# Group norm of an SSD scan: summed onto all partitions with a matrix of ones, in place of a column that is spread again

## Chip, cores and metric

One core of a Trainium2 chip. The metric is the device time of one execution in microseconds, median of several runs.

## What is computed

One step of a hybrid decoder layer: 512 prompt tokens and 8 single-token sequences go through a shared RMS norm and input projection, then through two branches, sparse attention and a Mamba-2 scan (SSD), then a gated merge and a feed-forward block. The change is in the scan branch. Its 2048 channels are eight groups of 256; each group's output is multiplied by a gate and then normalised over its own 256 channels:

```python
y = y.reshape(b, t, D_INNER) * jax.nn.silu(z.astype(F32))
yg = y.reshape(b, t, SSM_GROUPS, D_INNER // SSM_GROUPS)
yg = yg * lax.rsqrt(jnp.mean(yg * yg, axis=-1, keepdims=True) + EPS)
y = yg.reshape(b, t, D_INNER) * ssm_norm_w.astype(F32)
```

For the eight sequences a top-k of 256 out of 2049 scores is also needed; it has nothing to do with the scan, but VectorE does its 32 rounds in between.

## The kernel before

Everything is float32 and lies channels on partitions, the T = 520 tokens (512 + 8) in the free dimension. Each engine has its own program written out by hand, with semaphores between them; there is no scheduler, so the order of the lines in an engine's block is its order on the chip. S("name") is a semaphore; counters such as 4 * g + 3 are absolute.

The scan runs over groups g = 0 to 7. Group 0 and group 7 stand alone, 1 to 6 are a hardware loop (Fori). The pass of group g computes group g and, between, (a) the projection tiles of group g + 1 on TensorE: D(0) to D(5), each 128 output channels by 520 tokens over 8 blocks of input channels, 32 records in the profile (16 matmuls, of two records each), and (b) the norm of group g - 1. So seven passes hold a norm, and the eighth norm stands behind the scan.

The norm of a group, before: POOL adds the squares of the two 128-channel halves into sqg. TensorE (step_norm, sum_squares, L387) multiplies each block of tokens with a column of ones, which leaves the sums with tokens on partitions, 4 columns of 128 and one of 8, in PSUM bank 6. ScalarE takes the root of these five columns into rt (root_norm, L403), VectorE inverts them (recip_norm, L409). TensorE visits a second time and spreads them back over all partitions (spread_norm, L395 and L396), ScalarE copies that to rbg (copy_norm, L413 and L414), and VectorE multiplies Y with it (norm, L1651), which gives the group's two tiles of ssm_o.

Around it on TensorE: D(1), the spread, then step_turn, which transposes B (L900) and x (L905; it writes banks 6 and 7, in which the norm's sums lie), then D(2), step_decode (L917, for which it needs VectorE's xdt), D(3), step_cb (L925, C times B, which needs the end of VectorE's decode work on both halves), then the chunks of the scan (L934, L947, L950, L953) between D(4) and D(5). On VectorE, in order: the convolution, four silus (L1675), the reciprocal, MAX8 of a top-k round (L1627), the norm of group g - 1, xdt (L1686), xw, the rest of that round, the decode work (L1706 to L1720), and a second round.

Behind the scan, TensorE turns the state (L1002) and runs the SSM branch's projection over the sixteen tiles of ssm_o (sbr, L359); only its first tile waits for each ssm_o tile as it becomes ready. VectorE does the remaining 16 rounds of the top-k, with a gated product (gated, L1765) after every second one, and TensorE waits for the last round at L1038.

Of the kernel before, what the change touches and what calls it, by code (L numbers as in the profile page):

```python
# [76 lines left out]
def build(nc, x_prompt, x_sample, cache_k, cache_v, cache_idx_k, state_ssm, state_conv, page_table,  # L77
# [5 lines left out]
    with ExitStack() as ctx:  # L83
# [284 lines left out]
        def two(ap):  # L368

            return ap.rearrange("p (h t) -> p h t", h=2)  # L370
# [8 lines left out]

        NORM2, NORMF = NG + 1, NG + 2  # L380

        def sum_squares(pe, e, *squares):

            for b in range(5):
                n = P if b < 4 else NB
                for i, sq in enumerate(squares):
                    mm = pe.matmul(ps[0:n, 6, b:b + 1], sq[:, b * P:b * P + n], ones[:, 0:1],  # L387
                                   start=(i == 0), stop=(i == len(squares) - 1))
            mm.then_inc(S("norm_summed"), 1)
# [59 lines left out]
        def _(sp):  # L449
# [43 lines left out]

            sp.wait_ge(S("iktok_copied"), 2)
            sp.dma_start(ik_prompt[0, 0].rearrange("(b p) d -> p b d", p=P), iktok[:, 0:4, :]).then_inc(S("stored"), 16)
# [164 lines left out]
        def _(pe):  # L660
# [98 lines left out]
            with pe.Fori(0, 2) as k:  # L759
                for s in range(2):  # L760
                    pe.wait_ge(w_in_slot[s], 16 * k + 16)
                    for j in range(2):
                        dense(pe, 4 * k + N_IQ + 2 * s + j, j, block_of(s, j), xns)
            pe.wait_ge(S("ik_sq"), 1)
            for h in range(2):
# [74 lines left out]
            pe.wait_ge(S("kvtok_copied"), 5)  # L840
            pe.wait_ge(S("iktok_copied"), 2)
            pe.wait_ge(S("dense_read"), N_SSM)
# [47 lines left out]
            def step_norm(g):  # L890

                pe.wait_ge(S("sqg_added"), g + 1)
                sum_squares(pe, g + 1, sqg[:, 0, :])

            def step_turn(g, prev):

                pe.wait_ge(S("ctok_ready"), g + 1)
                pe.wait_ge(S("silu_done"), 4 * g + 3)
                for c in range(4):
                    pe.transpose(ps[:, 5, c * P:(c + 1) * P], xc[:, 2, c * P:(c + 1) * P], ident)  # L900
                if prev:
                    pe.wait_ge(S("norm_copied"), 2 * g + 2)
                for c in range(4):
                    for j in range(2):
                        mm = pe.transpose(ps[:, 6 + c // 2, (c % 2) * 256 + j * P:(c % 2) * 256 + (j + 1) * P],  # L905
                                          xc[:, j, c * P:(c + 1) * P], ident)
                mm.then_inc(S("turned"), 1)
# [48 lines left out]
            def group(g, prev, more):  # L956
                D = (lambda *a: group_tile(g + 1, *a)) if more else last_tile
                D(0, 0, 4)
                step_aux(g, prev)
                D(0, 4, 8)  # L960
                if prev:
                    step_norm(g - 1)
                D(1)
                if prev:
                    spread_norm(pe, g)
                step_turn(g, prev)
                D(2)
# [29 lines left out]
            step_norm(NG - 1)  # L997
            spread_norm(pe, NG)
            pe.wait_ge(S("h_done"), 4 * NG)
# [44 lines left out]

            pe.wait_ge(S("norm_copied"), 2 * NG + 2)
            pe.wait_ge(S("decode_read"), POS_READ)
# [104 lines left out]
        def _(act):  # L1151
# [18 lines left out]
            act.wait_ge(S("tensor_mark"), VECS_TURNED)  # L1170
            act.activation(vec[:, 0:72], ps[:, 4, 0:72], ACT.Copy).then_inc(S("vec_ready"), 1)
            copy_norm(act, 0, rbc)
            act.activation(taps, ps[:, 4, 128:256], ACT.Copy, scale=0.5).then_inc(S("taps_ready"), 1)
            act.activation(dsk, ps[:, 4, 256:272], ACT.Copy).then_inc(S("dsk_ready"), 1)
            act.wait_ge(S("dense_done"), 1)
# [7 lines left out]
            act.wait_ge(S("vector_mark"), IK_SQ_IN)  # L1183
            act.activation(ikt2, ikt1, ACT.Square).then_inc(S("ik_sq"), 1)
            with act.Fori(0, 4) as k:
# [5 lines left out]
            act.wait_ge(S("tensor_mark"), IK_VAR)  # L1191
            act.activation(two(ikt2), ps[:, 4:6, 0:TH], ACT.Sqrt, bias=eps[:, 0:1]).then_inc(S("ik_root"), 1)
            act.wait_ge(S("tensor_mark"), TOK_TURNED)
# [33 lines left out]
            act.wait_ge(S("dense_read"), N_SSM)  # L1227
            act.activation(qkvs[:, 0:8, :], uT[:, :, SEQ:T], ACT.Copy).then_inc(S("qkvs_ready"), 1)
            act.activation(qkvs[:, 8:12, :], kviq[:, 0:4, SEQ:T], ACT.Copy).then_inc(S("qkvs_ready"), 1)
            act.wait_ge(S("tensor_mark"), IK_TURNED)  # L1230
            act.activation(iktok[:, 0:4, :], ps[:, 4, 0:256].rearrange("p (b d) -> p b d", b=4), ACT.Copy).then_inc(S("iktok_copied"), 1)
            act.activation(iktok[0:NB, 4, :], ps[0:NB, 4, 256:320], ACT.Copy).then_inc(S("iktok_copied"), 1)
            for b in range(5):
# [62 lines left out]
            def squares(g):  # L1296
                for j in range(2):
                    act.wait_ge(S("Y_ready"), 2 * g + j + 1)
                    act.activation(sqg[:, j, :], Y[:, j, :], ACT.Square).then_inc(S("sqg_ready"), 1)

            def group(g, prev, more):
                for i in range(4):
# [25 lines left out]
                if prev:  # L1328
                    root_norm(act, g, 256)
                if more:  # L1330
                    tile_in(g + 1, 0)
                    tile_in(g + 1, 1)
                else:
                    gate_ahead(0)
                    gate_ahead(1)
                if prev:
                    copy_norm(act, g, rbg)
                act.wait_ge(S("turned"), g + 1)
# [27 lines left out]
            group(NG - 1, True, False)  # L1366
            root_norm(act, NG, 256)
            copy_norm(act, NG, rbg)
            act.wait_ge(S("aux_done"), NG + 1)
# [101 lines left out]
        def _(v):  # L1471
# [10 lines left out]
            v.wait_ge(S("vec_ready"), 1)  # L1482
            rms_dve(v, 0, 0, 0)
# [26 lines left out]
            for c in range(4):  # L1510
# [5 lines left out]
                                   ALU.mult, ALU.add).then_inc(S("vector_mark"), 1)  # L1516
            v.wait_ge(S("ik_root"), 1)
            chain(v.reciprocal(ikt2, ikt2))
# [121 lines left out]
            def z_gate(g):  # L1640

                for j in range(2):
# [3 lines left out]
                    v.scalar_tensor_tensor(z, thz[:, j, :], 1.0, z, ALU.add, ALU.mult).then_inc(S("z_ready"), 1)  # L1646

            def norm(g):
                v.wait_ge(S("norm_copied"), 2 * g + 4)
                for j in range(2):  # L1650
                    v.scalar_tensor_tensor(ssm_o[:, bass.ds(2 * g + j, 1), :].rearrange("p o t -> p (o t)"), Y[:, j, :],  # L1651
                                           cwg[:, bass.ds(g, 1), 22 + j:23 + j].rearrange("p o t -> p (o t)"), rbg,
                                           ALU.mult, ALU.mult).then_inc(S("ssm_ready"), 1)

            def group(g, prev, more):
# [21 lines left out]
                if prev:  # L1677
                    recip_norm(v, g)
                    top_max(GROUP_ROUNDS * g)
                    norm(g - 1)  # L1680
                else:
                    top_max(GROUP_ROUNDS * g)
# [73 lines left out]
            group(NG - 1, True, False)  # L1756
            recip_norm(v, NG)
            norm(NG - 1)


# [102 lines left out]
        def _(g):  # L1863

            g.wait_ge(S("vec_ready"), 1)
            g.wait_ge(S("taps_ready"), 1)
            g.wait_ge(S("dsk_ready"), 1)
            tp = taps.rearrange("p (t n) -> p n t", t=4)
# [156 lines left out]
```

## Time and profile before

| | |
|---|---|
| median of 3 runs | 1772.5 us (1771.49 to 1774.18) |
| the profiled execution: its time, its span | 1774.49 us, 1772.7 us |
| TensorE busy | 1681.0 us, 95% of the span |
| VectorE busy | 767.6 us, 43% |
| ScalarE busy | 401.1 us, 23% |
| GpSimd busy | 217.5 us, 12% |
| mean granted clock of TensorE | 0.96 |

Busy time is summed over the whole span. The scan lies at about 360 to 942 us; one pass takes about 71.4 us. In the rows below the first number is the start in us from the span's start, the second the time in us; "x32" counts records that were merged into one row, and a bracket gives the idle time of that engine ahead of the row and what ended it. PE is TensorE, DVE is VectorE, ACT is ScalarE.

### The profile page before, as it was taken

How to read it: one execution, taken by the hardware profiler on the slowest of the kernel's cores; microseconds unless marked ns; L12 is line 12 of the kernel's file. 1: busy time of each engine (PE TensorE's matmuls, PEld its weight loads, DVE VectorE, ACT ScalarE, POOL GpSimd, SP SyncE). 2: the span in 40 equal slices, each digit the busy share in tenths (PEclk: the TensorE clock that was granted, in tenths of full speed). 3: DMA queues.
4: the chain of work that ended last, by engine and by line, in shares of the span. 5: the costliest groups of instructions: out<-in, count | busy, mean ns of one | idle time of the engine just before them, and what ended most of it. 6: DMA issues, size and time to landing. Idle time of an engine off the chain costs nothing. (4 is left out here: it accounts for less than half of the span.)

```text
span 1772.7 us, 21861 instructions
## 1 busy us (share of the span) xinstructions
PE 1681.0 (95%) x8411; PEld 1426.5 (80%) x8411; DVE 767.6 (43%) x1192; ACT 401.1 (23%) x855; POOL 217.5 (12%) x224
## 2 busy tenths in 40 slices
PE   6998998999999999999999999999899999999997
PEld 5886786787877878777777888888788888888886
DVE  3314886166776866868657972011210001010002
ACT  3113226223333343343421000101111111110002
POOL 1000111013132241232310005100000000000000
PEclk8998989999999999999899999889899999999997
DMA  6111123223313222131223225112212222222201
GB/s 197 48 36 49 39 61 93 57 65 102 96 55 97 78 69 77 54 101 48 79 72 109 85 72 169 60 57 72 71 52 91 71 71 71 71 68 65 82 1 48
DMA packets 153482, 131.12 MB, mean 74 GB/s; under 512 B 11410, under 2 KB 149938, under 8 KB 153410
## 3 DMA queue, kind: packets, MB, share of 16 engines
q1 hardware_dynamic: 150610, 121.93, 22.7%
q0 software_dynamic: 2816, 8.39, 1.6%
q8 instruction: 42, 0.69, 0.2%
q14 instruction: 14, 0.11, 0.0%
HBM read 117.26 MB, written 13.27 MB: 74 GB/s over the span
## 5 line engine op out<-in xcount | busy, mean ns | idle before, releaser
L359 PE MATMUL ps<-xn,ring 128*128 128x260 f32 x4160 | 951.7, 388 | 7.6 <-DVE xn L442 3.3
L359 PEld LDWEIGHTS ps<-xn,ring 128*128 128x128 f32 x4160 | 793.7, 193 | 136.0 <-issue 3.8
L359 PE MATMUL ps<-work,ring 128*128 128x260 f32 x960 | 210.7, 382 | 0.0
L359 PEld LDWEIGHTS ps<-work,ring 128*128 128x128 f32 x960 | 182.4, 190 | 28.0
L359 PE MATMUL ps<-ssm_o,ring 128*128 128x260 f32 x512 | 114.0, 386 | 0.0
L359 PEld LDWEIGHTS ps<-ssm_o,ring 128*128 128x128 f32 x512 | 98.3, 192 | 15.3
L1834 DVE TENSOR_TENSOR xT<-xT,work 128x520 f32<-128x520 f32 x16 | 11.2, 701 | 192.3 <-ACT work L1434 192.3
L1941 POOL TENSOR_TENSOR ring<-ring 128x512 f32<-128x512 f32 x32 | 40.5, 1266 | 334.2 <-ACT ring L1294 334.2
L1848 DVE SCALAR_TENSOR_TENSOR work<-work 128x520 f32 (+1 forms) x22 | 15.4, 700 | 145.8 <-ACT work L1449 145.8
L1627 DVE MAX8 work<-work 8x8 f32<-8x2049 f32 x32 | 72.9, 2278 | 0.6
L1633 DVE FIND_INDEX8 dix<-work 8x8 uint32<-8x2049 f32 x32 | 72.8, 2274 | 0.0
L1636 DVE MATCH_REPLACE8 work<-work 8x2049 f32<-8x2049 f32 x32 | 72.5, 2267 | 0.0
L1852 DVE TENSOR_TENSOR work<-work 128x520 f32 (+1 forms) x22 | 15.4, 701 | 130.8 <-ACT work L1453 130.8
L1668 DVE SCALAR_TENSOR_TENSOR work<-work 128x512 f32<-128x512 f32 x96 | 67.0, 768 | 7.3 <-ACT work L1304 7.3
L359 PE MATMUL ps<-uT,ring 128*128 128x260 f32 x256 | 59.0, 395 | 0.4 <-DVE uT L1819 0.4
L1735 DVE TENSOR_TENSOR work<-work 128x256 f32<-128x256 f32 x24 | 18.0, 750 | 93.5 <-PE ps L953 93.5
L359 PEld LDWEIGHTS ps<-uT,ring 128*128 128x128 f32 x256 | 50.4, 197 | 8.7 <-DVE uT L1819 0.5
L1290 ACT ACTIVATE ring<-ps,work 128x128 f32<-128x128 f32 x128 | 36.6, 368 | 79.6 <-PE ps L934 79.6
L1434 ACT ACTIVATE work<-ps 128x520 f32<-128x520 f32 x16 | 9.7, 604 | 194.4 <-PE ps L359 194.4
L1264 ACT ACTIVATE work<-ps 128x520 f32<-128x520 f32 x32 | 18.2, 594 | 129.7 <-PE ps L359 129.7
L1453 ACT ACTIVATE work<-ps 128x520 f32<-128x520 f32 x22 | 13.3, 604 | 134.8 <-PE ps L359 134.8
L934 PEld LDWEIGHTS ps<-work,gs 32*128 32x128 f32 x256 | 30.8, 186 | 9.1 <-issue 8.1
(300 smaller groups left out, 1665.2 us busy)
## 6 DMA issues: line engine op xcount, KB each, us to landing
ring<-in_w_in SPq DMA_DIRECT2D x34, 1024.0 KB, 5.3
ring<-in_w_ffn_up SPq DMA_DIRECT2D x11, 1024.0 KB, 5.3
ring<-in_w_ffn_gate SPq DMA_DIRECT2D x11, 1024.0 KB, 5.3
ring<-in_w_in SPq DMA_DIRECT2D x16, 512.0 KB, 5.3
work<-in_state_ssm SPq DMA_DIRECT2D x16, 512.0 KB, 6.3
out<-work SPq DMA_DIRECT2D x16, 512.0 KB, 4.0
ring<-in_w_ssm_br SPq DMA_DIRECT2D x8, 1024.0 KB, 7.9
ring<-in_w_ffn_down SPq DMA_DIRECT2D x8, 1024.0 KB, 5.1
```

Of the source, the lines that this page charges most:

```text
L359: mm = pe.matmul(ps[0:m, 2 * pair + h, 0:TH], lhs[k], rhs[k][:, h * TH:(h + 1) * TH], start=(k == 0), stop=(k == len(lhs) - 1))
L934: mm = pe.matmul(ps[:, 4, r * P:(r + 1) * P], gs[:, r * P:(r + 1) * P], acT[0:32, c * P:(c + 1) * P], start=True, stop=True)
L1264: act.activation(two(raw[:, i, 3:T + 3]), tile_out(i % 2), ACT.Copy).then_inc(S("dense_read"), 1)
L1290: act.activation(M2[:, c % 2, r * P:(r + 1) * P], abc[:, r * P:(r + 1) * P], ACT.Relu, scale=-1.0, bias=atg[:, c, r:r + 1]).then_inc(S("E_ ...
L1627: v.max(dm8[0:NB, :], smp[0:NB, :]).then_inc(S("dtop_max"), 1)
L1633: v.max_index(dix[:], dm8[0:NB, :], smp[0:NB, :]).then_inc(S("dtop_index"), 1)
L1636: v.match_replace(smp[0:NB, :], dm8[0:NB, :], smp[0:NB, :], -3.3e38).then_inc(S("dtop_cut"), 1)
L1668: v.scalar_tensor_tensor(xc[:, i, 0:SEQ], raw[:, i, t:t + SEQ], cw[:, 5 * i + t:5 * i + t + 1], xc[:, i, 0:SEQ], ALU.mult, ALU.add).then_i ...
L1735: v.tensor_tensor(hT.rearrange("p (r q) -> p r q", q=64), hT.rearrange("p (r q) -> p r q", q=64), ealast[:, :, c:c + 1].broadcast_to((P, 4 ...
L1848: v.scalar_tensor_tensor(hs[j], gate[:, j, :], 1.0, hs[j], ALU.add, ALU.mult).then_inc(S("silu_h"), 1)
L1852: v.tensor_tensor(hs[j], hs[j], stage[:, j, :], ALU.mult).then_inc(S("hid_ready"), 1)
L1941: g.tensor_tensor(m, m, CBm[:, c:c + 1, :].broadcast_to((P, 4, P)), ALU.mult).then_inc(S("M_ready"), 1)
```

## The change

The sum of squares is made with the whole 128x128 matrix of ones as the stationary operand, which leaves each token's sum on all 128 partitions, 520 columns in banks 6 and 7. ScalarE takes the root of all 520 columns straight into rbg, VectorE inverts rbg in place, and the spreading and the two copies go. Turning x now waits for the root (group_root), since that frees banks 6 and 7. The norms outside the scan (root_norm, copy_norm, spread_norm with e = 0, NORM2, NORMF) stay as they were. Seven semaphores of the head, each raised by ScalarE, become one, head_read, with counts; that is shown once.

```diff
+        VEC_READY, TAPS_READY, DSK_READY, IK_SQ, IK_ROOT, QKVS_READY, IKTOK_READY = 1, 2, 3, 4, 5, 7, 9
-            v.wait_ge(S("ik_root"), 1)
+            v.wait_ge(S("head_read"), IK_ROOT)
...
             def step_norm(g):
 
                 pe.wait_ge(S("sqg_added"), g + 1)
-                sum_squares(pe, g + 1, sqg[:, 0, :])
+                for h in range(2):
+                    mm = pe.matmul(ps[:, 6 + h, 0:TH], ones, sqg[:, 0, h * TH:(h + 1) * TH], start=True, stop=True)
+                mm.then_inc(S("group_summed"), 1)
...
                 if prev:
-                    pe.wait_ge(S("norm_copied"), 2 * g + 2)
+                    pe.wait_ge(S("group_root"), g)
                 for c in range(4):
                     for j in range(2):
                         mm = pe.transpose(ps[:, 6 + c // 2, (c % 2) * 256 + j * P:(c % 2) * 256 + (j + 1) * P],
...
                 D(1)
-                if prev:
-                    spread_norm(pe, g)
                 step_turn(g, prev)
...
             step_norm(NG - 1)
-            spread_norm(pe, NG)
...
+            def group_norm(g):
+
+                act.wait_ge(S("group_summed"), g)
+                act.activation(two(rbg), ps[:, 6:8, 0:TH], ACT.Sqrt, scale=1.0 / 256,
+                               bias=eps[:, 0:1]).then_inc(S("group_root"), 1)
...
                 if prev:
-                    root_norm(act, g, 256)
+                    group_norm(g)
                 if more:
                     tile_in(g + 1, 0)
                     tile_in(g + 1, 1)
...
-                if prev:
-                    copy_norm(act, g, rbg)
                 act.wait_ge(S("turned"), g + 1)
...
+            def group_recip(g):
+                v.wait_ge(S("group_root"), g)
+                v.reciprocal(rbg, rbg).then_inc(S("group_recip"), 1)
+
             def norm(g):
-                v.wait_ge(S("norm_copied"), 2 * g + 4)
+                v.wait_ge(S("group_recip"), g + 1)
...
                 if prev:
-                    recip_norm(v, g)
+                    group_recip(g)
                     top_max(GROUP_ROUNDS * g)
                     norm(g - 1)
```

How the instructions stand on TensorE in a pass of the loop, from the second half of D(0) to the turning. Before (lines of the kernel before; L387 is the sum, L395 and L396 the spread, L900 and L905 the turning):

```order
L359 MATMUL ps<-xn,ring 128x260 x8
L387 MATMUL ps<-cst,work 128x1 x4
L387 MATMUL ps<-cst,work 8x1
L354 REGISTER_ALU
L359 MATMUL ps<-xn,ring 128x260 x16
L393 ISA
L395 MATMUL ps<-cst,rt 128x128 x4
L396 MATMUL ps<-cst,rt 128x8
L898 REGISTER_ALU
L900 MATMUL ps<-cst,work 128x128 x4
L905 MATMUL ps<-cst,work 128x128 x8
L808 ISA
```

And with the change, where L895 is the sum, L903 and L908 the turning:

```order
L360 MATMUL ps<-xn,ring 128x260 x8
L895 MATMUL ps<-work,cst 128x260 x2
L355 REGISTER_ALU
L360 MATMUL ps<-xn,ring 128x260 x16
L901 REGISTER_ALU
L903 MATMUL ps<-cst,work 128x128 x4
L908 MATMUL ps<-cst,work 128x128 x8
L809 ISA
```

Between D(1) and the turning nothing of the norm is left; the sum in front of D(1) has two instructions of 260 columns in place of five of one.

On VectorE in the same pass, from the silus to the norm. Before:

```order
L1675 SCALAR_TENSOR_TENSOR work<-work 128x520 x4
L409 RECIPROCAL rt<-rt 128x4
L409 RECIPROCAL rt<-rt 8x1
L1625 REGISTER_ALU
L1627 MAX work<-work 8x8
L1649 ISA
L1651 ISA
L1651 REGISTER_ALU
L1651 SCALAR_TENSOR_TENSOR ssm_o<-work,cwg 128x520
L1651 ISA
L1651 REGISTER_ALU
L1651 SCALAR_TENSOR_TENSOR ssm_o<-work,cwg 128x520
```

With the change (L1682 are the silus, L1653 is the reciprocal, L1630 MAX8, L1658 the norm):

```order
L1682 SCALAR_TENSOR_TENSOR work<-work 128x520 x4
L1653 RECIPROCAL work<-work 128x520
L1628 REGISTER_ALU
L1630 MAX work<-work 8x8
L1658 ISA x2
L1658 SCALAR_TENSOR_TENSOR ssm_o<-work,cwg 128x520
L1658 ISA
L1658 REGISTER_ALU
L1658 SCALAR_TENSOR_TENSOR ssm_o<-work,cwg 128x520
```

The reciprocal keeps its place, ahead of MAX8 and the norm, with xdt and xw behind those, and has 520 columns in place of four and one.

On TensorE behind the last group, from the last tile of the scan to the top-k's transposes (L1038 in both). Before:

```order
L359 MATMUL ps<-xn,ring 128x260 x6
L387 MATMUL ps<-cst,work 128x1 x4
L387 MATMUL ps<-cst,work 8x1
L395 MATMUL ps<-cst,rt 128x128 x4
L396 MATMUL ps<-cst,rt 128x8
L1002 MATMUL ps<-cst,work 128x128 x2
L359 MATMUL ps<-ssm_o,ring 128x260 x192
L359 MATMUL ps<-xn,ring 128x260 x32
L359 MATMUL ps<-ssm_o,ring 128x260 x64
L1038 MATMUL ps<-cst,work 128x8 x2
```

With the change:

```order
L360 MATMUL ps<-xn,ring 128x260 x6
L895 MATMUL ps<-work,cst 128x260 x2
L1002 MATMUL ps<-cst,work 128x128 x2
L360 MATMUL ps<-ssm_o,ring 128x260 x192
L360 MATMUL ps<-xn,ring 128x260 x32
L360 MATMUL ps<-ssm_o,ring 128x260 x64
L1038 MATMUL ps<-cst,work 128x8 x2
```

The state's transposes (L1002) and the projection over ssm_o follow the sum directly.

## Rows read from the trace of the kernel before

**Rows 1.** TensorE's timeline in a middle pass: start, us, line, records, idle before.

```profile
653.53 7.28 PE L359 MATMUL ps<-xn,ring 128*128 128x260 f32 x32
663.91 1.16 PE L395 MATMUL ps<-cst,rt 128*128 128x128 f32 x8 [3.10 <-DVE rt L409]
...
666.22 1.91 PE L905 MATMUL ps<-cst,work 128*128 128x128 f32 x8
667.93 7.58 PE L359 MATMUL ps<-xn,ring 128*128 128x260 f32 x32
...
686.37 1.16 PE L925 MATMUL ps<-work 128*128 128x128 f32 x8 [0.27 <-DVE ring L1717]
```

**Rows 2.** ScalarE's timeline in that pass, the root.

```profile
661.92 1.28 ACT L403 ACT_TABLE_LOAD   x1
663.21 0.40 ACT L403 ACTIVATE rt<-ps,eps 128x4 f32<-128x4 f32 x2
```

**Rows 3.** VectorE's timeline in that pass, from the reciprocal to the decode work.

```profile
663.64 0.21 DVE L409 RECIPROCAL rt<-rt 128x4 f32<-128x4 f32 x2 [1.12 <-ACT rt L403]
663.85 2.28 DVE L1627 MAX8 work<-work 8x8 f32<-8x2049 f32 x1
666.37 1.43 DVE L1651 SCALAR_TENSOR_TENSOR ssm_o<-work,cwg 128x520 f32 x2 [0.24 <-ACT work L414]
668.17 1.29 DVE L1686 TENSOR_TENSOR xdt<-ps,work 128x512 f32<-128x512 f32 x2 [0.37 <-PE ps L905]
...
677.40 1.23 DVE L1706 TENSOR_TENSOR ring<-ps,work 128x1024 f32<-128x1024 f32 x1 [1.93 <-PE ps L917]
```

**Rows 4.** Answers on lines L1192 and L1518, both in the head.

```profile
L1192 ACT ACTIVATE work<-ps,eps x1: 695/695/695, 106.3 to 106.3; 128x520 f32<-128x520 f32 x1
...
L1518 DVE RECIPROCAL work<-work x1: 3403/3403/3403, 107.0 to 107.0; 128x520 f32<-128x520 f32 x1
```

**Rows 5.** VectorE's timeline, first and last pass with a norm.

```profile
451.05 2.28 DVE L1627 MAX8 work<-work 8x8 f32<-8x2049 f32 x1
453.56 1.43 DVE L1651 SCALAR_TENSOR_TENSOR ssm_o<-work,cwg 128x520 f32 x2 [0.23 <-ACT work L414]
...
463.32 1.22 DVE L1706 TENSOR_TENSOR ring<-ps,work 128x1024 f32<-128x1024 f32 x1 [1.13 <-PE ps L917]
...
878.31 2.27 DVE L1627 MAX8 work<-work 8x8 f32<-8x2049 f32 x1
...
894.11 1.23 DVE L1706 TENSOR_TENSOR ring<-ps,work 128x1024 f32<-128x1024 f32 x1 [3.65 <-PE ps L917]
```

**Rows 6.** Windows of 3.5 us; TensorE's granted clock is third from the end.

```profile
451.00:454.50 3.50, 3.23 (x24) 2.83 (x25) 3.27 (x5) 1.48 (x5) 0.00 (x0) 1.00 0.92 297
664.50:668.00 3.50, 3.50 (x21) 3.25 (x20) 3.06 (x3) 0.74 (x3) 0.00 (x0) 0.62 0.29 98
880.50:884.00 3.50, 2.84 (x12) 2.65 (x12) 2.34 (x5) 1.20 (x4) 0.00 (x0) 0.50 0.00 0
```

**Rows 7.** TensorE's timeline: D(0)'s second half, and waits for the reciprocal.

```profile
436.22 5.36 PE L359 MATMUL ps<-xn,ring 128*128 128x260 f32 x16
...
451.10 1.16 PE L395 MATMUL ps<-cst,rt 128*128 128x128 f32 x8 [1.40 <-DVE rt L409]
...
649.02 3.67 PE L359 MATMUL ps<-xn,ring 128*128 128x260 f32 x16
...
878.44 1.16 PE L395 MATMUL ps<-cst,rt 128*128 128x128 f32 x8 [1.42 <-DVE rt L409]
```

**Rows 8.** TensorE's timeline behind the last group.

```profile
937.27 1.18 PE L387 MATMUL ps<-cst,work 128*128 128x1 f32 x10 [3.06 <-POOL work L1908]
...
942.20 18.10 PE L359 MATMUL ps<-ssm_o,ring 128*128 128x260 f32 x75
...
1071.77 0.29 PE L1038 MATMUL ps<-cst,work 8*128 8x8 f32 x2 [1.67 <-DVE work L1638]
```

**Rows 9.** VectorE's timeline behind the last group.

```profile
1056.74 0.70 DVE L1765 SCALAR_TENSOR_TENSOR work<-work 128x520 f32<-128x520 f32 x1 [8.79 <-ACT work L1384]
```

More of the change, by code:

```diff
@@ L375, in block_of @@
             return [ring[:, slot, k, j * P:(j + 1) * P] for k in range(kt)]
-        NORM2, NORMF = NG + 1, NG + 2
+        NORM2, NORMF = 1, 2
         def sum_squares(pe, e, *squares):
@@ L492, in _ @@
             sp.dma_start(smp[0:NB, 0:PAST], scratch).then_inc(S("smp_in"), 16)
-            sp.wait_ge(S("iktok_copied"), 2)
+            sp.wait_ge(S("head_read"), IKTOK_READY)
             sp.dma_start(ik_prompt[0, 0].rearrange("(b p) d -> p b d", p=P), iktok[:, 0:4, :]).then_inc(S("stored"), 16)
@@ L763, in _ @@
                         dense(pe, 4 * k + N_IQ + 2 * s + j, j, block_of(s, j), xns)
-            pe.wait_ge(S("ik_sq"), 1)
+            pe.wait_ge(S("head_read"), IK_SQ)
             for h in range(2):
@@ L840, in _ @@
             pe.wait_ge(S("kvtok_copied"), 5)
-            pe.wait_ge(S("iktok_copied"), 2)
+            pe.wait_ge(S("head_read"), IKTOK_READY)
             pe.wait_ge(S("dense_read"), N_SSM)
@@ L1043, in _ @@
             ga(2, 0)
-            pe.wait_ge(S("norm_copied"), 2 * NG + 2)
+            pe.wait_ge(S("group_root"), NG)
             pe.wait_ge(S("decode_read"), POS_READ)
@@ L1170, in _ @@
             act.wait_ge(S("tensor_mark"), VECS_TURNED)
-            act.activation(vec[:, 0:72], ps[:, 4, 0:72], ACT.Copy).then_inc(S("vec_ready"), 1)
+            act.activation(vec[:, 0:72], ps[:, 4, 0:72], ACT.Copy).then_inc(S("head_read"), 1)
             copy_norm(act, 0, rbc)
-            act.activation(taps, ps[:, 4, 128:256], ACT.Copy, scale=0.5).then_inc(S("taps_ready"), 1)
-            act.activation(dsk, ps[:, 4, 256:272], ACT.Copy).then_inc(S("dsk_ready"), 1)
+            act.activation(taps, ps[:, 4, 128:256], ACT.Copy, scale=0.5).then_inc(S("head_read"), 1)
+            act.activation(dsk, ps[:, 4, 256:272], ACT.Copy).then_inc(S("head_read"), 1)
             act.wait_ge(S("dense_done"), 1)
@@ L1183, in _ @@
             act.wait_ge(S("vector_mark"), IK_SQ_IN)
-            act.activation(ikt2, ikt1, ACT.Square).then_inc(S("ik_sq"), 1)
+            act.activation(ikt2, ikt1, ACT.Square).then_inc(S("head_read"), 1)
             with act.Fori(0, 4) as k:
@@ L1191, in _ @@
             act.wait_ge(S("tensor_mark"), IK_VAR)
-            act.activation(two(ikt2), ps[:, 4:6, 0:TH], ACT.Sqrt, bias=eps[:, 0:1]).then_inc(S("ik_root"), 1)
+            act.activation(two(ikt2), ps[:, 4:6, 0:TH], ACT.Sqrt, bias=eps[:, 0:1]).then_inc(S("head_read"), 1)
             act.wait_ge(S("tensor_mark"), TOK_TURNED)
@@ L1227, in _ @@
             act.wait_ge(S("dense_read"), N_SSM)
-            act.activation(qkvs[:, 0:8, :], uT[:, :, SEQ:T], ACT.Copy).then_inc(S("qkvs_ready"), 1)
-            act.activation(qkvs[:, 8:12, :], kviq[:, 0:4, SEQ:T], ACT.Copy).then_inc(S("qkvs_ready"), 1)
+            act.activation(qkvs[:, 0:8, :], uT[:, :, SEQ:T], ACT.Copy).then_inc(S("head_read"), 1)
+            act.activation(qkvs[:, 8:12, :], kviq[:, 0:4, SEQ:T], ACT.Copy).then_inc(S("head_read"), 1)
             act.wait_ge(S("tensor_mark"), IK_TURNED)
-            act.activation(iktok[:, 0:4, :], ps[:, 4, 0:256].rearrange("p (b d) -> p b d", b=4), ACT.Copy).then_inc(S("iktok_copied"), 1)
-            act.activation(iktok[0:NB, 4, :], ps[0:NB, 4, 256:320], ACT.Copy).then_inc(S("iktok_copied"), 1)
+            act.activation(iktok[:, 0:4, :], ps[:, 4, 0:256].rearrange("p (b d) -> p b d", b=4), ACT.Copy).then_inc(S("head_read"), 1)
+            act.activation(iktok[0:NB, 4, :], ps[0:NB, 4, 256:320], ACT.Copy).then_inc(S("head_read"), 1)
             for b in range(5):
@@ L1366, in _ @@
             group(NG - 1, True, False)
-            root_norm(act, NG, 256)
-            copy_norm(act, NG, rbg)
+            group_norm(NG)
             act.wait_ge(S("aux_done"), NG + 1)
@@ L1481, in _ @@
                 v.tensor_reduce(dst, src.rearrange("p k t -> p t k"), AX.X, ALU.add).then_inc(S("squares_added"), 1)
-            v.wait_ge(S("vec_ready"), 1)
+            v.wait_ge(S("head_read"), VEC_READY)
             rms_dve(v, 0, 0, 0)
@@ L1756, in _ @@
             group(NG - 1, True, False)
-            recip_norm(v, NG)
+            group_recip(NG)
             norm(NG - 1)
@@ L1863, in _ @@
         def _(g):
-            g.wait_ge(S("vec_ready"), 1)
-            g.wait_ge(S("taps_ready"), 1)
-            g.wait_ge(S("dsk_ready"), 1)
+            g.wait_ge(S("head_read"), VEC_READY)
+            g.wait_ge(S("head_read"), TAPS_READY)
+            g.wait_ge(S("head_read"), DSK_READY)
             tp = taps.rearrange("p (t n) -> p n t", t=4)
```

## The prediction

> **What bounds the kernel now.** I read the page first, then TensorE's timeline for one pass of the scan loop, then the lists of ScalarE and VectorE beside it, and last the timeline behind the scan. By the page TensorE is busy in 95% of the span, so a reader would first count its columns. A middle pass shows why that isn't enough. In the pass whose norm falls at 663 us, the tile D(1) ends at 660.81 (653.53 + 7.28) and TensorE stands idle 3.10 us, until VectorE has inverted the five small columns of roots [rows 1]. What it waited for is a chain on other engines: a table load of 1.28 us, two roots, 0.40 us together, up to 663.61 [rows 2], two reciprocals in 0.21 us [rows 3]. Then TensorE spreads the columns from 663.91, turns B, turns x from 666.22, and D(2) starts at 667.93.
>
> The second place is C*B at L925 (686.37) [rows 1]. VectorE has had gaps of 0.24, 0.37 and 1.93 us by then, together 2.54, all spent waiting for TensorE or what hangs on it [rows 3]; from L1706 at 677.40 to L925 lie 8.97 us of VectorE's decode work without a gap, and TensorE waits 0.27 us for its end [rows 1, 3]. So the two engines hold each other here: TensorE sets when L1706 begins, VectorE sets when L925 begins. A change that frees TensorE alone can gain nothing at L925 unless L1706 starts earlier too.
>
> **The change, part by part, for a middle pass.**
>
> *Sum.* Five sums of one column, ten records, become two products of 260 columns, four records. A record of that width takes 0.23 us (7.28 / 32 in [rows 1]), so 0.91 us; the tail's ten records took 1.18 [rows 8], so about 0.2 us is saved. In the loop that only lengthens the wait behind D(1), and is worth nothing.
>
> *Root.* One root over 520 columns read from PSUM took 0.70 us in the head, at L1192 [rows 4]. It replaces 0.40 us, in the same place behind the same table load: it ends at 663.21 + 0.70 = 663.91, later by 0.30. The two copies of the spread norm go; nobody waits for them any more.
>
> *Spread.* Ten records and the 3.10 us wait before them go. Turning B waits only for the third silu, which ScalarE's table load follows, and finishes under the root. Turning x starts at the root's end, about 664.0. It took 1.71 us before (666.22 to 667.93), so D(2) starts near 665.7, **2.2 us earlier**.
>
> *Reciprocal.* It now runs over 128x520. VectorE has that very shape once in the head: 3.40 us [rows 4], against 0.21. MAX8, the previous group's norm, xdt, xw and one round of the decode top-k are queued behind it on VectorE. They are **3.19 + 0.30 = 3.49 us later** at MAX8. xdt is ready near 672.3, before D(2) ends (673 or, at the lower clock, 674), so L917 isn't held.
>
> The Trainium skill ("VectorE: DVE Perf Modes", First, the fixed hardware budget) says that Reciprocal runs an iterative divide with a repeat count of 8. Taken as eight times a plain operation on 520 columns (half of the norm's 1.43 us in [rows 3]) that is an estimate of 5.7 us a reciprocal, 2.3 more in each of seven passes, 16 us more in the sum; the row of the same shape decides against that reading, so the sum stays with 3.40.
>
> *What the pass gets.* Without its gaps, the stretch from MAX8 to L1706 is 12.27 - 1.36 = 10.91 us in the first pass with a norm, where the gaps were 0.23 and 1.13 [rows 5]. Now 3.49 + 10.91 = 14.40 must fit. In the middle pass it was 13.55 (663.85 to 677.40), so L1706 and with it L925 come **0.85 us later**. The five middle passes are alike within 0.2 us (the third is shown). In the first pass it was 12.27: 2.13 later. In the last, where TensorE ran slowly, 15.80 (878.31 to 894.11): 1.40 earlier [rows 5]. Sum: 2.13 + 5 x 0.85 - 1.40 = **+5.0 us**. TensorE's 2.2 us turn into idle time before L925: 0.27 + 2.2 + 0.85 = 3.3 us. From L925 to the group's last product it is TensorE that sets the time, so the delay is passed on in full.
>
> *Tail.* After the last group TensorE did its sum at 937.27, waited, spread, turned the state and began the SSM projection at 942.20 [rows 8]. Now sum (0.9) and turning (0.6) leave it at 938.9, since the projection asks for the last two normed tiles only after fourteen others, over 12 us of work; root and reciprocal hide under them. **3.3 us earlier.** That is kept: VectorE's rounds wait there for TensorE, 8.79 us at 1056.74 [rows 9], and their last result lets TensorE go on at 1071.77 [rows 8], so both move together.
>
> *The clock.* In the middle pass the granted clock is 0.62 from 664.5 to 668.0 (most of it at the lower level, 1.2 GHz), after 3.10 us of idling [rows 1, 6]; in the first pass, after 1.40 us, it stays 1.00, and in the last, after 1.42 us and small work, it is 0.50 [rows 6, 7]. The new idle time before L925 is 3.3 us if the clock was full until then, and about 2.2 if it had already fallen at the turning (the slow part costs D(2) some 1.2 us, which VectorE hides). After L925 nothing hides it. The price of one low stretch is in two rows for the same sixteen records: 5.36 against 3.67 us, 1.69 us [rows 7]. Some of a stretch falls into idle time; I take 1.4 us, in five of seven passes: **+7 us**. Bounds: 0, and 7 x 1.69 = 11.8.
>
> The Trainium skill ("TensorE: Matmul & The Clock Gate", HAM oscillation — how this bites in real kernels) warns that idle gaps between bursts put the array back to its slow state, once in each pass. The trace agrees at the gap of 3.10 us. By it, with every pass caught, the sum would be 11.8 instead of 7; that end is in my range.
>
> The semaphores joined into one in the head order the same events on the same engines; I cost them at nothing, since ScalarE raises it in its program order. If a waiter there had to wait for a later step, it would show before 100 us.
>
> **Sum.** +5.0 - 3.3 + 7 = +8.7 us, so the profiled 1774.5 us become 1783.2. That execution is 2.0 us above the median of the runs, 1772.5; on the median I forecast **1781 us**. This kernel's measurement tells about 0.2% (3.5 us) from no change.
>
> **Rivals.**
> - *The clock holds at L925.* Then only +5.0 - 3.3 = +1.7: 1774.2 on the median, no change to be measured. For it: a wait of 1.40 us in the loop, and one of 1.67 in the tail [rows 7, 8], are short beside 3.10, and the new one lies between. Against it: the last pass, where 1.42 us and small work were enough. 23%.
> - *VectorE isn't the one that counts, and the freed TensorE time is kept* (the other side). This needs a reciprocal that adds less than the gaps hold: 13.55 - 10.91 = 2.64 us in a middle pass, less 0.30 for the root, so 2.55 us in all where 0.21 stood; below that the pass gets shorter. With one near zero cost each pass would gain up to 2.2: 7 x 2.2 + 3.3 = 18.7 us, 1754. Against it stand two reciprocals of 520 columns at 3.4 us. 10%, with halfway cases.
> - *Every pass is caught, and the tail too.* The tail's early start falls into a slow stretch and gives back what such a stretch costs, 1.7: 5.0 - 1.6 + 11.8 = +15.2, 1787.7. 12%.
> - *The forecast* (the clock falls behind the new wait in three to six passes, which is 1.7 + 4.2 to 1.7 + 10.1 us, 1778 to 1784): 55%.
>
> **Range.** From 1774, which takes in most of the second case, to 1787. The likeliest case alone, with 1 us of scatter on either side: 1777 to 1785. Faster by over 0.2% (under 1769): 0.10, the third case. Within 0.2%: the clock case but for its top, 0.21. Slower (above 1776): the rest, 0.69.
>
> **What the changed profile would show.** The reciprocal at 3.4 us, eight times; MAX8 3.5 us later against the exponential before it; no gap of VectorE before L1706's successor; TensorE with about 1 + 1.5 us idle around the turning of B and 2 to 3.3 us before C*B, released by VectorE; the granted clock right behind C*B at 1.00 or near 0.5, and with it the sixteen records of the first half of D(4) at 3.7 or 5.4 us; the projection starting some 1.6 us after the last sum begins. I am wrong if the reciprocal is much shorter than in the head, or if the decode product of TensorE, not VectorE, still releases L1706's successor.

## The result and the profile after

The changed kernel takes **1796.6 us** (median of 4 runs, 1791.2 to 1797.2) against 1773.0 us (4 runs): 1.0127 times the time of before, 95% interval 1.0105 to 1.0149. Forecast were 1781 us and at most 1787. The sign and the mechanism named as likeliest were right, the size wasn't: 23.7 us lost, not 8. The profiled execution has a span of 1794.3 us, 21.6 more than before.

TensorE's timeline in a middle pass of the changed kernel, to be held against [rows 1] (L903 turns B, L908 turns x, L928 is C*B, L937 is L934 of before, L950 is L947):

```profile
665.70 7.18 PE L360 MATMUL ps<-xn,ring 128*128 128x260 f32 x32
674.02 0.66 PE L903 MATMUL ps<-cst,work 128*128 128x128 f32 x4 [1.14 <-DVE work L1682]
676.25 1.67 PE L908 MATMUL ps<-cst,work 128*128 128x128 f32 x8 [1.58 <-ACT work L1304]
677.71 8.32 PE L360 MATMUL ps<-xn,ring 128*128 128x260 f32 x32
...
699.30 1.16 PE L928 MATMUL ps<-work 128*128 128x128 f32 x8 [2.67 <-DVE ring L1724]
700.38 1.99 PE L937 MATMUL ps<-work,gs 32*128 32x128 f32 x8
702.30 6.24 PE L360 MATMUL ps<-xn,ring 128*128 128x260 f32 x16
```

The wait of 3.10 us for the reciprocal and the spread are gone. Two waits around the turning took their place, 1.14 and 1.58 us. And C*B, which waited 0.27 us, now waits 2.67. Right behind it the sixteen records of D(4)'s first half take 6.24 us; in the kernel before they took 3.77 in this place.

VectorE's timeline in the same pass, against [rows 3] (L1653 reciprocal, L1630 MAX8, L1658 norm, L1693 xdt, L1713 the decode work), and below it ScalarE's root (L1304), against [rows 2]:

```profile
676.23 3.40 DVE L1653 RECIPROCAL work<-work 128x520 f32<-128x520 f32 x1 [1.41 <-ACT work L1304]
679.55 2.23 DVE L1630 MAX8 work<-work 8x8 f32<-8x2049 f32 x1
681.70 1.40 DVE L1658 SCALAR_TENSOR_TENSOR ssm_o<-work,cwg 128x520 f32 x2
683.03 1.27 DVE L1693 TENSOR_TENSOR xdt<-ps,work 128x512 f32<-128x512 f32 x2
...
690.33 1.23 DVE L1713 TENSOR_TENSOR ring<-ps,work 128x1024 f32<-128x1024 f32 x1
```

```profile
674.21 1.28 ACT L1304 ACT_TABLE_LOAD   x1
675.50 0.69 ACT L1304 ACTIVATE work<-ps,eps 128x520 f32<-128x520 f32 x1
```

Every step of the forecast's VectorE chain is here: 3.40 us of reciprocal, 0.69 of root, and no bracket on any row down to L1713: VectorE no longer waits, it is the one that is waited for.

Windows over the wait and what follows (third number from the end is the granted clock):

```profile
696.00:699.30 3.30, 0.62 (x4) 0.20 (x2) 3.13 (x4) 0.60 (x1) 0.00 (x0) 1.00 0.85 237
699.30:702.70 3.40, 3.40 (x17) 3.06 (x18) 3.40 (x3) 0.29 (x2) 0.00 (x0) 0.68 1.05 276
702.70:706.10 3.40, 3.40 (x9) 2.63 (x9) 3.22 (x5) 3.25 (x7) 0.04 (x1) 0.50 1.19 288
706.10:709.50 3.40, 3.40 (x17) 2.62 (x15) 2.14 (x2) 0.00 (x0) 1.22 (x1) 0.82 0.53 131
709.50:713.00 3.50, 3.50 (x18) 2.96 (x16) 0.00 (x0) 2.15 (x6) 1.11 (x1) 1.00 0.00 0
```

While TensorE idles in this pass the clock is still at 1.00; it falls some 1.2 us after it works again, and is back only near 707.3, in the middle of the dense tile D(4). What is missing to 1.00 adds up: (0.32 + 0.50 + 0.18) x 3.4 = 3.4 us of TensorE time. The passes can be measured from C*B to the fourth chunk's product, which has the same short wait of about 1.1 us for VectorE ahead of it in both kernels. Before, that was 26.04 us in six passes (as 472.29 to 498.33). TensorE's rows of after:

```profile
471.92 2.07 PE L928 MATMUL ps<-work 128*128 128x128 f32 x8 [4.03 <-DVE ring L1724]
501.12 0.45 PE L950 MATMUL ps<-ring,xdt 128*64 128x128 f32 x4 [1.11 <-DVE work L1745]
547.12 2.07 PE L928 MATMUL ps<-work 128*128 128x128 f32 x8 [4.03 <-DVE ring L1724]
577.95 0.45 PE L950 MATMUL ps<-ring,xdt 128*64 128x128 f32 x4 [1.11 <-DVE work L1745]
...
962.66 1.15 PE L895 MATMUL ps<-work,cst 128*128 128x260 f32 x4 [1.60 <-POOL work L1915]
...
963.86 11.34 PE L360 MATMUL ps<-ssm_o,ring 128*128 128x260 f32 x51
...
1091.93 0.29 PE L1038 MATMUL ps<-cst,work 8*128 8x8 f32 x2 [1.67 <-DVE work L1641]
```

It is 29.2 to 30.8 us in the first six passes; the last has a distance of its own (28.4 against 25.2). The span's 21.6 us divide so:

| from ... to | before and after, us | difference |
|---|---|---|
| start to the fourth chunk's product of group 0 | 428.20, 425.92 | -2.3 |
| from there to C*B, seven passes | sum | +3.4 |
| C*B to the fourth chunk's product, seven passes | sum | +24.3 |
| last of these to L1038 in the tail | 143.5, 138.3 | -5.2 |
| behind L1038 | 700.9, 702.4 | +1.4 |

The second row is VectorE's part: from the fourth chunk's product to the next C*B it takes 46.0 us in each of the seven passes of the changed kernel, and took 44.1 in the first, 45.3 to 45.6 in the middle and 47.5 in the last before. The first row holds nothing of the group norm, only the seven joined semaphores; the last lies behind all changes. The first is partly scatter: five traces of the experiments below whose kernels are unchanged up to this point from the kernel before reach it at 426.4 to 428.0 us.

### The profile page after: what moved, and what is told of

It reads as the page before. It is cut to its first block and busy times, and to the rows that moved or that the text cites. A ratio compares the mean times of both kernels' runs of the same rounds, so it can differ in the third digit from the quotient of the medians.

```text
span 1794.3 us, 21567 instructions
## 1 busy us (share of the span) xinstructions
PE 1688.6 (94%) x8283; PEld 1428.1 (80%) x8283; DVE 790.2 (44%) x1184; ACT 397.6 (22%) x831; POOL 217.3 (12%) x224
## 5 line engine op out<-in xcount | busy, mean ns | idle before, releaser
L360 PE MATMUL ps<-xn,ring 128*128 128x260 f32 x4160 | 970.3, 394 | 8.5 <-DVE xn L443 3.3
L360 PEld LDWEIGHTS ps<-xn,ring 128*128 128x128 f32 x4160 | 807.5, 196 | 143.9 <-issue 6.4
L1630 DVE MAX8 work<-work 8x8 f32<-8x2049 f32 x32 | 72.5, 2266 | 0.5
L937 PEld LDWEIGHTS ps<-work,gs 32*128 32x128 f32 x256 | 36.1, 214 | 9.6 <-issue 9.2
```

Source lines behind the costliest of these rows:

```text
L360: mm = pe.matmul(ps[0:m, 2 * pair + h, 0:TH], lhs[k], rhs[k][:, h * TH:(h + 1) * TH], start=(k == 0), stop=(k == len(lhs) - 1))
L937: mm = pe.matmul(ps[:, 4, r * P:(r + 1) * P], gs[:, r * P:(r + 1) * P], acT[0:32, c * P:(c + 1) * P], start=True, stop=True)
L1630: v.max(dm8[0:NB, :], smp[0:NB, :]).then_inc(S("dtop_max"), 1)
```

## The experiments

The theory was now: **the clock behind C*B** costs 3.3 us a pass and VectorE's later reciprocal the rest. The rival: something else behind C*B, or the reciprocal by itself, costs it. Each ratio is against the kernel before on the same chip.

**1. Fill the wait.**

```diff
 def step_cb(g):
+    pe.wait_ge(S("dense_read"), 6 * g + N_SSM + 9)
+    for i in range(5):
+        pe.matmul(ps[:, 0, 0:TH], ident, xns[i % KT][:, 0:TH], start=True, stop=True)
     pe.wait_ge(S("C_used"), 2 * g + 2)
```

> The changed kernel with five products of 260 columns (ten records, about 2.3 us) put ahead of the wait before C*B in every pass; their result is overwritten, so they are pure filler. Clock theory: TensorE no longer idles 2.7 to 4.0 us there, the granted clock stays at 1.00 behind C*B, and each of seven passes gets back about 3.3 us: 1796.6 - 23 = about 1773 us (1771 to 1778). Rival (the time behind C*B is lost by something other than idling in front of it, such as later data or contention): the filler gains nothing, 1796 to 1800 us, and the first half of D(4) still takes 6.2 us.

1775.0 us, 1.0016 (1.0002 to 1.0031). Work that is of no use to anyone takes 21.6 us off the changed kernel. TensorE's timeline with it (L928 the filler, L931 C*B, L953 the fourth chunk's product):

```profile
688.03 2.35 PE L928 MATMUL ps<-xn,cst 128*128 128x260 f32 x10
692.22 1.16 PE L931 MATMUL ps<-work 128*128 128x128 f32 x8 [1.83 <-DVE ring L1727]
693.31 1.15 PE L940 MATMUL ps<-work,gs 32*128 32x128 f32 x8
694.39 3.77 PE L360 MATMUL ps<-xn,ring 128*128 128x260 f32 x16
...
718.26 0.45 PE L953 MATMUL ps<-ring,xdt 128*64 128x128 f32 x4 [1.11 <-DVE work L1748]
```

3.77 us, and 26.04 from C*B to the chunk, in the first six passes alike. The loss behind C*B is the clock's, and it comes from idling ahead of it. The filler didn't take the whole wait away: 1.83 us are left in three of the passes, and the clock held behind those.

**2. The kernel before, with the reciprocal's load on VectorE.**

```diff
     recip_norm(v, g)
+    v.reciprocal(sqg[:, 1, :], sqg[:, 1, :])
     top_max(GROUP_ROUNDS * g)
```

> The kernel before, with one more reciprocal of 520 columns on VectorE (into a buffer that is free then) behind the two small ones in the loop's seven passes. VectorE is 3.4 us later, TensorE's part is unchanged. Clock theory: L1706 and C*B come later by 3.4 less the gaps (2.1, five times 0.8, and 0 us), the wait before C*B grows only from 0.3 to about 1.1 us, so the clock doesn't fall behind it: 1773 + 6 = about 1779 us, and the first half of D(4) stays at 3.8 us. Rival (a reciprocal of this width in this place is what costs 3.3 us a pass, by itself): 1773 + 24 = about 1797 us.

Median 1785.3 us over ten runs, 1.0074 (1.0042 to 1.0106), but no run is near it: five lie at 1775.8 to 1777.9 and five at 1792.8 to 1795.8. The profiled execution (span 1774.0) is of the lower group, where the clock theory put all of them. Its rows:

```profile
544.16 1.16 PE L925 MATMUL ps<-work 128*128 128x128 f32 x8 [2.00 <-DVE ring L1718]
...
546.33 3.77 PE L359 MATMUL ps<-xn,ring 128*128 128x260 f32 x16
...
570.20 0.45 PE L947 MATMUL ps<-ring,xdt 128*64 128x128 f32 x4 [1.10 <-DVE work L1739]
```

C*B comes later by 3.4 us over the seven passes, where the expectation had 6; the waits ahead of it are 2.0 us in the first two passes and 0.3 to 0.8 in the others, and the clock held even behind those of 2.0 us. The upper group has no trace, but every run has its mean granted clock: 0.951 to 0.954 in the five upper runs, 0.961 to 0.963 in the five lower ones. 0.01 of 1790 us is 18 us, about the distance of the groups. So the upper group is a lower clock; where in the pass it falls there isn't shown by this.

**3. The same kernel once more**, for an execution of the upper group.

> The kernel before with the extra reciprocal once more, for a profile of an execution from the upper group (1793 to 1796 us). Clock theory: in it the granted clock is near 0.5 right behind C*B in every pass and the distance from C*B to the fourth chunk's product is 29.3 us in place of 26.0; an execution of the lower group shows 26.0.

Eight runs, four at 1772.6 to 1777.2 and four at 1792.2 to 1793.2. The profiled one (span 1770.8) fell into the lower group again, so the upper group's trace wasn't seen. The granted clocks divide as before: 0.953 to 0.954 above, 0.963 to 0.965 below.

**4. The same kernel, with three filler products.**

> The kernel before with the extra reciprocal of 520 columns, whose runs fell into two groups, 1776 to 1778 and 1793 to 1796 us, now with three filler products (1.4 us) ahead of the wait before C*B. If the upper group is the clock that falls behind a wait of 0.6 to 2.0 us, it goes: all runs at 1775 to 1779 us. If the two groups have another cause, both stay.

The edit is that of experiment 1 with three products. All eight runs lie at 1775.3 to 1780.6 us, 1.0031 (1.0019 to 1.0044). The upper group is gone, and the granted clock is 0.962 to 0.965 in all eight. A filler ahead of C*B removed it, so the group hangs on that wait; that the clock fell right behind it, as in the changed kernel, is the likely reading, without a trace of it.

**5. More load on VectorE in the kernel before**, so that the wait grows to that of the changed kernel.

```diff
     v.reciprocal(sqg[:, 1, :], sqg[:, 1, :])
+    v.reciprocal(thz[:, 0, 0:256], thz[:, 0, 0:256]) if more else None
```

> The kernel before with the extra reciprocal of 520 columns and, in six of the seven passes, one more of 256 columns (about 1.7 us) behind it, so that VectorE brings C*B late by about 2.5 us in a middle pass and TensorE waits some 2.7 us ahead of it, as long as in the changed kernel, while the old norm with its second visit stays. Chain alone: 1777 + 6 x 1.7 = 1787 us. Clock theory: the clock falls behind that wait in nearly every pass as well, 3.3 us each: 1806 to 1811 us, all runs in one group, and the first half of D(4) takes 6 us. If the fall needs something of the changed kernel, it stays at 1787 us with that half at 3.8 us.

1800.6 us (1795.7 and 1805.4), 1.0155 (1.0089 to 1.0221): more than the chain alone gives, less than the clock in every pass. With two runs 10 us apart the size is uncertain. The old norm is in this kernel, and the fall behind C*B too, in the first, third and fifth of the seven passes:

```profile
475.46 2.08 PE L925 MATMUL ps<-work 128*128 128x128 f32 x8 [3.62 <-DVE ring L1719]
505.71 0.45 PE L947 MATMUL ps<-ring,xdt 128*64 128x128 f32 x4 [1.10 <-DVE work L1740]
...
553.15 1.16 PE L925 MATMUL ps<-work 128*128 128x128 f32 x8 [0.77 <-DVE ring L1719]
579.18 0.45 PE L947 MATMUL ps<-ring,xdt 128*64 128x128 f32 x4 [1.10 <-DVE work L1740]
```

30.25 us behind a wait of 3.62, 26.03 behind one of 0.77. The waits of 0.8 us are in the second, fourth and sixth pass, in which the clock had fallen at the spread for long (0.50 from 528.7 to 535.5 us, twice as long as in the third) and slowed the work that fills the time up to C*B. I had counted on a long wait in each.

**6. Two filler products in place of five in the changed kernel.**

> The changed kernel with two filler products (0.9 us) ahead of the wait before C*B in place of five. The wait shrinks from 2.7 to 4.0 us to about 1.8 to 3.1 us. If the clock falls behind some of these waits and not behind others, the time lies between 1775 and 1797 us, or its runs fall into groups; if it needs the whole wait, all runs are at 1775 us, if any wait will do, all at 1797 us.

1795.7 us (1794.1 to 1796.8), 1.0127 (1.0110 to 1.0144): nothing gained. The waits didn't all become shorter: they are 3.15, 1.80, 1.80, 1.82, 3.15, 3.14 and 2.33 us, since where the clock no longer fell at the turning, TensorE came to C*B earlier and waited longer. Its timeline (L931 is C*B) says more than its time:

```profile
625.92 1.16 PE L931 MATMUL ps<-work 128*128 128x128 f32 x8 [1.80 <-DVE ring L1727]
655.24 0.45 PE L953 MATMUL ps<-ring,xdt 128*64 128x128 f32 x4 [1.11 <-DVE work L1748]
...
701.24 1.16 PE L931 MATMUL ps<-work 128*128 128x128 f32 x8 [1.82 <-DVE ring L1727]
727.28 0.45 PE L953 MATMUL ps<-ring,xdt 128*64 128x128 f32 x4 [1.11 <-DVE work L1748]
```

The same wait, 1.80 and 1.82 us, is followed by 29.32 us once and by 26.04 the next time; the other six passes were all caught. The length of a wait alone doesn't decide it.

**7. A short reciprocal.** The changed kernel, inverting 64 of the 520 columns; the other 456 stay uninverted.

```diff
-    v.reciprocal(rbg, rbg).then_inc(S("group_recip"), 1)
+    v.reciprocal(rbg[:, 0:64], rbg[:, 0:64]).then_inc(S("group_recip"), 1)
```

> The changed kernel with the reciprocal over 64 of the 520 columns only; it leaves the other 456 columns uninverted. The reciprocal takes about 0.45 us in place of 3.4. My own rival case of the forecast (TensorE's freed time is kept once VectorE is short): L1706 is set by TensorE again, C*B comes about 2.2 us earlier than before, the wait ahead of it is back at 0.3 us and the clock holds: 1773 - 7 x 2.2 - 5 = about 1753 us. If VectorE's length isn't what counts, it stays near 1797 us.

1760.5 us, 0.9930 (0.9913 to 0.9946). With VectorE short the change is a gain, so the reciprocal's length is what turns it. It missed 1753 in part because C*B still waits 1.50 us for VectorE in five passes, and the clock fell behind that in two of them. One is the first pair below, 29.36 us; the other, at 538.86, took 27.67 us and so cost 1.6 us and not 3.3, with the same work behind it:

```profile
678.87 1.16 PE L928 MATMUL ps<-work 128*128 128x128 f32 x8 [1.50 <-DVE ring L1724]
708.23 0.45 PE L950 MATMUL ps<-ring,xdt 128*64 128x128 f32 x4 [1.11 <-DVE work L1745]
...
821.01 1.16 PE L928 MATMUL ps<-work 128*128 128x128 f32 x8 [1.50 <-DVE ring L1724]
847.04 0.45 PE L950 MATMUL ps<-ring,xdt 128*64 128x128 f32 x4 [1.10 <-DVE work L1745]
```

**8. The tail alone.** The kernel before in the loop; sum, root and reciprocal of the changed one only behind the last group:

```diff
-            step_norm(NG - 1)
-            spread_norm(pe, NG)
+            tail_sum()
...
-            root_norm(act, NG, 256)
-            copy_norm(act, NG, rbg)
+            act.wait_ge(S("norm_summed"), NG + 1)
+            act.activation(two(rbg), ps[:, 6:8, 0:TH], ACT.Sqrt, scale=1.0 / 256,
+                           bias=eps[:, 0:1]).then_inc(S("norm_root"), 2)
...
-            recip_norm(v, NG)
+            v.wait_ge(S("norm_root"), 2 * NG + 2)
+            v.reciprocal(rbg, rbg).then_inc(S("norm_copied"), 2)
```

tail_sum() is the changed kernel's pair of products with ones.

> The kernel before in all seven passes of the loop; only the norm behind the last group is done the new way (ones matrix, root and reciprocal over 520 columns, no second visit). Forecast's tail term: 3.3 us less than before, and by the two traces up to 5.2 us, since the slow clock ends sooner: 1768 to 1770 us. Rival (the tail's gain is given back at the wait for the last top-k round): 1773 us.

1769.5 us, 0.9984 (0.9974 to 0.9993): 3.5 us less in the medians (the interval is 1.2 to 4.6). The forecast's tail term was 3.3; it isn't given back at the wait for the last round.

**9. The full reciprocal, but later on VectorE.**

```diff
-                if prev:
-                    group_recip(g)
-                    top_max(GROUP_ROUNDS * g)
-                    norm(g - 1)
-                else:
-                    top_max(GROUP_ROUNDS * g)
+                top_max(GROUP_ROUNDS * g)
...
                 for c in range(4):
                     if c == 3 and more:
                         z_gate(g + 1)
+                    if c == 1 and prev:
+                        group_recip(g)
+                        norm(g - 1)
                     v.wait_ge(S("y_done"), 4 * g + c + 1)
```

> The changed kernel with VectorE's reciprocal over 520 columns and the norm behind it moved, in the pass, from ahead of xdt to the wait for the second chunk's product (6.07 us of idle VectorE against 3.40 + 1.43 us). Forecast's steps: nothing of the norm is left between the silus and L1706, so TensorE's freed 2.2 us a pass are kept, C*B comes 2.2 us earlier than in the kernel before, and the wait ahead of it is 1.5 us or less. Chain theory alone: 1773 - 7 x 2.2 - 3.5 = 1754 us; with the clock falling behind C*B in one or two of seven passes, as with the short reciprocal, 1757 to 1762 us. If the reciprocal costs by its length wherever it stands, it stays above 1780 us.

**1746.2 us** (1744.3 to 1747.6), 0.9853 (0.9834 to 0.9872), the best of all, together with experiment 12. VectorE's timeline in a middle pass (L1708 the decode work, L1740 the second chunk's update), and TensorE's in another:

```profile
664.55 1.23 DVE L1708 TENSOR_TENSOR ring<-ps,work 128x1024 f32<-128x1024 f32 x1 [2.37 <-PE ps L920]
...
685.85 3.39 DVE L1653 RECIPROCAL work<-work 128x520 f32<-128x520 f32 x1
689.54 1.43 DVE L1658 SCALAR_TENSOR_TENSOR ssm_o<-work,cwg 128x520 f32 x2 [0.30 <-DVE work L1653]
692.00 0.42 DVE L1740 TENSOR_TENSOR work<-work 128x256 f32<-128x256 f32 x1 [1.02 <-PE ps L956]
```

```profile
535.94 1.16 PE L928 MATMUL ps<-work 128*128 128x128 f32 x8 [0.28 <-DVE ring L1719]
561.97 0.45 PE L950 MATMUL ps<-ring,xdt 128*64 128x128 f32 x4 [1.11 <-DVE work L1743]
...
569.99 5.36 PE L360 MATMUL ps<-xn,ring 128*128 128x260 f32 x16
```

The same 3.39 us and the norm behind them now end 1.02 us before the next product is there, TensorE releases VectorE at L1708 again (2.37), C*B waits 0.28, and behind each C*B the clock holds. It is some 8 us better than the chain gave, and that part is luck. The clock still falls once in a pass, but in most passes it does so in the second half of D(0), 5.36 us in place of 3.67, and no longer at the turning (x turned in 1.09 us there, where [rows 1] has 1.91). A slow D(0) leaves less to wait for at the turning, and such a pass takes 68.0 us; the one middle pass with the fall at the turning takes 69.6. Nothing in the edit was meant to move the fall.

**10. The norm later in the kernel before.** Only norm(g - 1) is moved to the same place.

> The kernel before with only VectorE's norm of the previous group (1.43 us) moved to the wait for the second chunk's product; the reciprocal of five columns and the spread stay. If the gain of the later reciprocal (1746 us) is owed to the order on VectorE, this gains too, up to 7 x 1.4 = 10 us: 1763 us. If it is owed to TensorE's removed second visit, which this kernel keeps, L1706 is still released by TensorE and nothing changes: 1770 to 1774 us.

1772.0 us, 0.9996 (0.9986 to 1.0006): nothing. So the order on VectorE isn't what gained in experiment 9; it let the removed second visit count.

**11. Useful work ahead of C*B.**

```diff
-                step_cb(g)
-                step_a(g, 0)
-                D(4, 0, 4)
-                step_a(g, 1)
-                D(4, 4, 8)
+                D(4, 0, 4)
+                step_cb(g)
+                step_a(g, 0)
+                D(4, 4, 6)
+                step_a(g, 1)
+                D(4, 6, 8)
```

> The changed kernel with the first half of D(4), sixteen records or 3.7 us of useful work, put ahead of C*B in place of behind it, and the rest split 2 and 2. Clock theory: the wait ahead of C*B (2.7 to 4.0 us) is filled, the clock stays at 1.00 behind it, C*B itself comes up to 1 us later: 1796.6 - 23 - 7 x 2 = 1760 us at best, 1772 us if the chunks' exponentials then hold TensorE. Without any clock effect only the moved 2.7 us would count: about 1778 us.

1766.6 us (1764.7 to 1767.9), 0.9964 (0.9952 to 0.9977). The wait ahead of C*B is 0.5 us and the whole loss is made good, but a wait of 1.19 us for ScalarE's exponentials is new in each pass, in the second row, as feared. The clock holds right behind C*B and falls behind this new wait instead, once in each pass: it is 0.53 from 695.2 to 698.8, and eight records take 3.13 us in the third row, where eight took 2.02 just before:

```profile
688.20 1.16 PE L928 MATMUL ps<-work 128*128 128x128 f32 x8 [0.52 <-DVE ring L1725]
693.59 1.15 PE L937 MATMUL ps<-work,gs 32*128 32x128 f32 x8 [1.19 <-ACT ring L1293]
694.67 3.13 PE L360 MATMUL ps<-xn,ring 128*128 128x260 f32 x8
```

**12. Both**: experiment 9 with a quarter of D(4) (eight records) ahead of C*B.

> Both edits: the reciprocal and norm later on VectorE, and a quarter of D(4) (eight records, 1.8 us) ahead of C*B. If the two losses are separate (VectorE's queue, and the clock behind the wait), this is the best of all: 1750 to 1756 us, with a scatter between runs of under 4 us. If the wait ahead of C*B is short already, it gains nothing over the later reciprocal alone.

1746.3 us (1745.9 to 1748.9), 0.9857 (0.9839 to 0.9875): no better than experiment 9 alone. Where no wait is left, there is nothing to fill.

## Why the prediction was wrong, step by step

- **Sum, root, spread, turning**: right. The root took 0.69 us. D(2) started 2.2 us behind the root's start (677.71 and 675.50), where 2.5 were forecast, and TensorE had 1.14 and 1.58 us of idle time around the turning of B, where I had said about 1 and 1.5.
- **Reciprocal and VectorE's queue**: right in kind, 3.4 us in the seven passes where the sum had +5.0. MAX8 came 3.41 us later and not 3.49, measured from the fourth chunk's product (641.01 to 663.85 before, 653.30 to 679.55 after), and MAX8 to L1713 took 10.78 us, not 10.91; these 0.2 us a pass are nearly the whole difference. VectorE is the engine that C*B waits for, shown by experiments 7 and 9.
- **"TensorE's 2.2 us turn into idle time before L925: 3.3 us"**: right in kind. With 2.2 us for a pass in which the clock had already fallen, the forecast was 2.2 to 3.3; the waits are 4.03, 4.03, 2.67, 2.67, 2.69, 2.75 and 3.20 us.
- **"After L925 nothing hides it"**: right, and shown: filler gave 21.6 us back.
- **"I take 1.4 us, in five of seven passes: +7 us. Bounds: 0, and 7 x 1.69"**: this is the step that failed, and the only one that put the result outside the range. The fall came in seven of seven passes and cost 3.3 us in most of them and 4.8 in one, 24.3 us together. I had taken the price of a fall from one row, the D(0) of [rows 7] (1.69 us), and made it the upper bound. Behind C*B the granted clock was missing 3.4 us' worth, twice that price: the slow stretch lasts twice as long. The kernel before had such a stretch as well: at 0.50 in [rows 6] and on into the group's D(2), which took 9.29 us in that pass in place of 7.58:

```profile
882.92 9.29 PE L359 MATMUL ps<-xn,ring 128*128 128x260 f32 x32
```

So the upper bound should have been two such prices, 7 x 3.4 = 24 us, which is about what was measured. Why the stretch is short in one place and long in another isn't shown. That small products stand behind C*B, where D(0) is dense, doesn't settle it: in experiment 7 the same small products followed a fall of 1.6 us and one of 3.3. The Trainium skill ("TensorE: Matmul & The Clock Gate", HAM oscillation — how this bites in real kernels) warned that a loop can pay the fall in every pass; the trace agrees, seven of seven.
- **Tail**: -3.3 was right, -3.5 by experiment 8; the -5.2 of the two traces is more than that, and the clock covers the rest: on this stretch it was missing 5.1 us' worth before (0.70 from 928.28 to 945.30) and 3.1 after (0.51 from 953.67 to 960.00).
- **The joined semaphores** weren't tried by themselves. The end of group 0 comes at 425.9 to 426.5 us in the three traces with the joined semaphores and an unchanged group 0 (the changed kernel, experiments 7 and 9), and at 426.4 to 428.2 in the six without them, so no added cost is seen, but no run isolates them.
- Of the rivals, the third (every pass caught) was the right one for the loop, with a price half of the true one; the part of it that gave back the tail's gain did not come. The second (VectorE doesn't count) fell with the result itself, where VectorE has no gap up to L1713; that a short reciprocal would make the change a gain is borne out by experiment 7.

What stays open is what decides whether a pass is caught. The same kernel (experiments 2 and 3) has two groups of times, nine runs and nine, some 16 to 18 us and 0.01 of granted clock apart, and the upper group's trace wasn't seen. Waits of 1.80 us were followed by a fall and waits of 1.83 us weren't. In the changed kernel all passes were caught, one after another, and I can only argue that a caught pass moves the next one into the same position. The trace agrees with it: in the third to seventh pass the clock falls 1.5, 1.2, 1.0, 0.8 and 0.5 us behind the start of C*B, nearly the same place each time (in the first two, behind waits of 4.03 us, just ahead of it). But no experiment varied that.

## What to carry to other kernels

Before a step is made wider to save another engine a visit, look at who is waited for next: here two engines took turns at holding each other, and freeing the one gave nothing as long as the other's work, 3.2 us longer, stood ahead of the point where they meet. Ask of every long operation who needs its result first. The normed tiles were needed only behind the scan, so the reciprocal belonged into a later wait of VectorE; the same instructions, moved, turned +1.3% into -1.5%.

An idle stretch of TensorE of some 1.5 to 4 us can cost twice: itself, and the slower clock of the work behind it, here 3.3 us most times, 1.6 once and up to 4.8. It need not: waits of 1.5 to 2.0 us also passed without a fall. Price it by the longest slow stretch in the trace, and take every pass being caught as a case of its own: here all seven were in one kernel, six, three or two in others, and none in some. Filling the wait, even with useless products, is a quick test for it.

## What was not expected of the hardware

A single kernel whose runs split in two groups, 1772.6 to 1777.9 and 1792.2 to 1795.8 us, nine and nine, with the upper group gone when each pass had 1.4 us of filler in a wait. And a granted clock that stays at 1.00 through a wait of 2.67 us, falls behind it (0.68 in the first 3.4 us, then 0.50, then 0.82), and returns only 8 us after the wait ended, though TensorE was busy all that time: the penalty lies not in the wait, where one looks, but in the rows after it.
